# The experts' result rows, stored by ScalarE's DMA queue two units later instead of by GpSimd's

## The reference, cut to what matters

```python
def _hier_moe(h, w_rg, b_rg, w_re, b_re, w1, w3, w2):
    ...
    e_id = g_top[:, None] * EXPERTS_PER_GROUP + top_j
    combine = jnp.einsum('nk,nke->ne', w_sel,
                         jax.nn.one_hot(e_id, N_EXPERTS, dtype=jnp.float32)).astype(h.dtype)
    y = jnp.zeros_like(hf)
    for e in range(N_EXPERTS):
        he = jax.nn.silu(hf @ w1[e]) * (hf @ w3[e])
        y = y + combine[:, e:e + 1] * (he @ w2[e])
    return y.reshape(B, S, D)

    # in second_block:
    x = x + g2[:, None, :] * _hier_moe(h2, w_rg[l], b_rg[l], w_re[l], b_re[l], w1[l], w3[l], w2[l])
```

## Time and profile before

| | us |
|---|---|
| median of 3 runs | 2029.37 |
| lowest and highest | 2022.58 and 2034.13 |
| the profiled execution's own time | 2036.26 |
| its span in the trace | 2034.5 |
| TensorE busy in the span | 1849.5 |
| the experts' stage, first group load to the last gather | about 1737 to 2026 |

### The profile page before, as it was taken

One profiled execution on the slowest core, in us unless ns is written; L12 is line 12 of the kernel. 1 busy time (PEld: TensorE's weight loads), 2 busy tenths in 40 slices (PEclk: granted clock), 3 DMA queues, 4 the chain that ended last, 5 costly groups with the idle time before them and its releaser, 6 DMA issues.

```text
span 2034.5 us, 16531 instructions
## 1 busy us (share of the span) xinstructions
PE 1849.5 (91%) x6558; PEld 1022.6 (50%) x6558; DVE 730.0 (36%) x1289; ACT 246.5 (12%) x519; POOL 114.3 (6%) x121
## 2 busy tenths in 40 slices
PE   6999879989999999998899989999798667799997
PEld 1454368644555444446455768844474554233332
DVE  0384253346677201022322256500336854211112
ACT  2000221110000000001022211100121130101110
POOL 0000000010000000001000000000202210100001
PEclk9999965799999999999756799999899768799999
DMA  9353400023646421127100048944342313999997
GB/s 347 123 194 137 167 21 1 0 103 124 223 170 227 165 83 65 59 83 269 57 0 1 1 148 326 332 165 155 82 166 83 114 60 127 352 391 387 390 392 283
DMA packets 160684, 334.45 MB, mean 164 GB/s; under 512 B 15192, under 2 KB 15472, under 8 KB 160608
## 3 DMA queue, kind: packets, MB, share of 16 engines
q1 hardware_dynamic: 141408, 298.87, 40.3%
q0 software_dynamic: 18288, 31.37, 4.8%
q10 hardware_dynamic: 912, 3.17, 0.4%
HBM read 355.58 MB, written 15.48 MB: 182 GB/s over the span
## 4 chain that ended last, share of the span: by engine, by line
PE 82%; DVE 9%; DMA 3%; issue 2%; ACT 2%; POOL 1%; SPq 0%; DVEq 0%; POOLq 0%; ACTq 0%
PE psum L535 79%; PE psum L539 4%; DMA wring<-in_w_mod 1%; POOL small L1220 1%; ACT big L1351 1%; DMA y_slots<-lnb 1%; DMA wring<-in_mlp_w 1%; ACT wide L1351 1%; DVE big L1875 0%; DVE small L1729 0%; DVE xres L1736 0%; DVE big L2015 0%; DVE big L2034 0%; DVE wide L1700 0%; DVE small L2033 0%
## 5 line engine op out<-in xcount | busy, mean ns | idle before, releaser
L535 PE MATMUL psum<-wring,big 128*128 128x512 f32 (+1 forms) x1536 | 559.4, 598 | 13.0 <-issue 10.2
L535 PE MATMUL psum<-wide,wring 128*128 128x256 f32 (+1 forms) x1520 | 513.8, 486 | 5.0 <-DVE wide L1700 5.0
L535 PEld LDWEIGHTS psum<-wring,big 128*128 128x128 f32 (+1 forms) x1536 | 231.6, 173 | 326.1 <-issue 326.1
L535 PEld LDWEIGHTS psum<-wide,wring 128*128 128x128 f32 x1520 | 276.2, 190 | 131.9 <-issue 112.0
L1662 DVE SCALAR_TENSOR_TENSOR wide<-wring,csilu,wide 128x512 f32<-128x512 f32 x364 | 250.4, 749 | 3.0
L535 PE MATMUL psum<-wring,wide 128*128 128x512 f32 (+2 forms) x512 | 208.2, 554 | 0.0
L535 PE MATMUL psum<-big 128*128 128x64 f32 (+3 forms) x480 | 131.6, 451 | 27.7 <-DVE big L1932 9.1
L1714 DVE TENSOR_TENSOR wide<-psum,gate 128x512 f32<-128x512 f32 x28 | 19.4, 692 | 377.9 <-PE psum L535 377.9
L535 PE MATMUL psum<-big,wide 128*64 128x512 f32 (+2 forms) x568 | 137.0, 544 | 3.9 <-DVE wide L1798 3.9
L535 PEld LDWEIGHTS psum<-const,wide 128*128 128x128 f32 x480 | 88.8, 199 | 95.3 <-issue 85.1
L1351 ACT ACTIVATE big<-psum 128x512 f32<-128x512 f32 (+1 forms) x141 | 76.1, 541 | 490.3 <-PE psum L535 369.7
(11 more groups left out here) (252 smaller groups left out, 1026.2 us busy)
## 6 DMA issues: line engine op xcount, KB each, us to landing
wring<-in_mlp_w SPq DMA_DIRECT2D x32, 2048.0 KB, 8.1
wring<-in_w SPq DMA_DIRECT2D x32, 2048.0 KB, 21.2
wring<-in_w_mod SPq DMA_DIRECT2D x24, 2048.0 KB, 10.2
big<-in_w SPq DMA_DIRECT2D x23, 2048.0 KB, 20.7
wide<-in_w SPq DMA_DIRECT2D x14, 2048.0 KB
wring<-in_w_ada SPq DMA_DIRECT2D x12, 2048.0 KB, 8.8
wring<-in_w_in SPq DMA_DIRECT2D x8, 2048.0 KB, 8.4
wring<-in_ev_w_in SPq DMA_DIRECT2D x6, 2048.0 KB, 13.5
```

The costliest lines, as they stand in the source:

```text
L535: return nc.tensor.matmul(o, a, b, start=first, stop=last)
```

## The change

The store leaves GpSimd's program and stands in ScalarE's, after the Silu of place i and for place i-2. GpSimd is left with the 12 group loads one after the other, the wait for all stores and the four gathers. The view that is stored, the semaphores and the number of stores (21) stay.

```diff
@@ GpSimd @@
-            begins = sorted(BEGINS)
-            loaded = 0
-            for i in range(UNITS - LATE):
-                while loaded < GROUPS and (loaded < 2 or begins[loaded - 2] <= i + 1):
-                    load_group(loaded)
-                    loaded += 1
-                u = ORDER[i]
-                pool.wait_ge(ysb_ready, i + 1)
-                pool.dma_start(y_slots[u * SLOTS:(u + 1) * SLOTS, :].rearrange("s (n c) -> n s c", n=2),
-                               ysb[:, i % 2, :]).then_inc(y_stored[i % 2], 16)
-            assert loaded == GROUPS
+            for n in range(GROUPS):
+                load_group(n)
             for a in range(2):
                 pool.wait_ge(y_stored[a], 16 * ((UNITS - LATE + 1 - a) // 2))
@@ ScalarE @@
+            def store_y(i):
+                u = ORDER[i]
+                act.wait_ge(ysb_ready, i + 1)
+                act.dma_start(y_slots[u * SLOTS:(u + 1) * SLOTS, :].rearrange("s (n c) -> n s c", n=2),
+                              ysb[:, i % 2, :]).then_inc(y_stored[i % 2], 16)
+
             act.wait_ge(pick_turned, 1)
...
                 act.wait_ge(up_done, i + 1)
                 f(sg[:, i % 2, :], psum[:, i % 2, 0:T], ACT.Silu).then_inc(sg_ready, 1)
+                if i > 1:
+                    store_y(i - 2)
                 if i + 1 in BEGINS:
                     modulate_group(BEGINS[i + 1])
```

## The result

| | before | after |
|---|---|---|
| median of 4 runs, us | 2029.86 | 2112.93 |
| lowest and highest | 2022.58, 2034.13 | 2098.50, 2122.75 |
| profiled execution, own time | 2036.26 | 2122.75 |
| its span | 2034.5 | 2120.9 |

The ratio is 1.0407, with a 95% interval of 1.034 to 1.0475: 83 us slower, where 98 were forecast. Ratios in this document leave out executions in a slow state of the chip; that is one of all, of 6354.78 us, in the run with GpSimd's late stores. The two profiled executions are 86.4 us apart in their spans. Of this the experts' stage begins 1.2 us later, which the change has no part in: the first group load is issued at 1738.08, before at 1736.91.

A forecast was written before the change was run, and what follows sets the result against it. DMA engines, mostly moving weights, and TensorE were both nearly used up. The pair's extra load +92.7, less 2.7, tail +8, made +98 on the profiled 2036.3 us; median forecast 2127 us, range 2085 to 2155.

The forecast's parts named there:

- The bound: Experts' stage: DMA engines and TensorE both nearly used up; work added to one or two DMA engines counts in full.
- Two engines, always the same pair: Stores on ScalarE's queue: outer dimension 2 gives two DMA engines, the same every time; chance 0.80, 2127 us.
- GpSimd's and ScalarE's sides: Experts' stage: GpSimd loses 21 issues, worth 0; ScalarE's 21 waits and issues of 0.41 to 1.59 us are hidden, 0.
- Rival (b): ScalarE's store issues are blocked while SyncE's queue is full: 24 us in all, 2053; chance 0.03.
- VectorE's side: `keep_y` waits for store i-2 with 14.5 us left: 0; in mid-stage a late store delays only VectorE.
- The sum: Experts' stage: net 2.26 MB more on the pair at 24.4 GB/s, +92.7 us, less 2.7 saved on GpSimd's queue: +90.
- The tail: After the last Silu: the last store lands late on the pair, gathers begin at T+12.4 instead of T+4.1: +8 us.
- (a): ScalarE's stores move round or spread over all sixteen engines: -1 to +2 us, 2026 to 2030; chance 0.13.
- (c): The pair is fixed, but has spare speed when fourteen engines idle, or gets less load: 2085 to 2105; chance 0.04.

The follow-up runs named there:

- the run with GpSimd's late stores: Kernel before, stores still on GpSimd's queue, but each waits until `up` of two units later is done: 2033.2 us, ratio 1.0048.
- The series 2, 4, 8, 64: Changed kernel, store's outer dimension 2 (ratio 1.0407), 4 (1.0207; forecast extra 40 us, less 3), 8 (1.0032; forecast 14, less 3), 64 as two DMAs (0.9966).
- the windows at the quiet end: Kernel before, its two output stores at outer dimension 2; profiled: both on ScalarE's queue 2055.1 us, ScalarE's plus SyncE's 2054.2, both on GpSimd's 2030.5.
- the run with halves: Changed kernel, each store still on ScalarE's queue but issued as two DMAs of 64 partitions: 2021.2 us, ratio 0.9966 to before.
- The two output stores on GpSimd's queue: Kernel before, its two output stores given outer dimension 2 and issued by GpSimd's queue: 2030.5 us in the profiled execution.

## Why the prediction was right, and where it was off

*The bound.* Right. What was left of the weights at 2090 lay on the pair; work on two engines counted almost in full while the mean share fell to 0.80.

*Two engines, always the same pair.* Right, and that it is the same pair could only be bounded before. The series 2, 4, 8, 64 and the windows at the quiet end show both halves. One reading behind it was weaker than it looked: I gave the share of 0.14 in the window 2014 to 2015 to the store alone. The DMA view of that microsecond splits it into 7.5% for GpSimd's queue and 7.0% for weights:

```profile
q0 software_dynamic: 15, 0.03, 7.5%
q1 hardware_dynamic: 8, 0.03, 7.0%
```

The count of two engines held, but that window couldn't prove it for a store; the quiet end of the kernel does.

*GpSimd's and ScalarE's sides.* Right at 0 for ScalarE: its issues took 0.50 us, and doubling their number cost nothing that can be measured. The free group loads gained nothing visible. Rival (b) is out by the row of ScalarE's issues: an issue is not held up although SyncE's take 9.4 us at the median.

*VectorE's side.* The cost was right, its reason was not. I expected a store to land in 8 to 13 us, inside 14.5. Fourteen of the 21 stores kept VectorE waiting for its buffer, and from their issue to the end of that wait it was 17.3 to 21.3 us. For store 19, issued at 2080.24, the chain has it:

```profile
2080.24 17.28 DMA y_slots<-lnb
```

The equal packet counts at 2090 explain most of it. While weights are queued, a store's 131,072 bytes on an engine pass together with twice as many of weights: 3 x 131,072 bytes at 25.6 GB/s are 15.4 us, an estimate from the rows above. VectorE waited 87.2 us. It cost nothing in the middle for the other reason that I had given: TensorE waited longer for weights.

*The sum: the term that was mis-sized is the pair's speed.* Expected +90 to the end of the last Silu, measured +77.7. I let the pair run at 24.4 GB/s an engine, a sixteenth of 390. Alone it makes 26 (0.13 and 52 GB/s above). In the stage the pair moved by my count 5.42 + 2.26 MB in 222.4 + 77.7 = 300.1 us: 25.6 GB/s, and somewhat more if the last w1 and w3 landed well ahead of 2083.45. The same speed puts four engines at (5.42+0.98)/25.6 = 250 us, +28, and eight at +3. Measured are +32.6 and +4.8 in the length of the stage. Of my 40 and 14, less 3 each, it is nearer for eight; for four it is as far below as 37 is above. The period points the same way: 49.4 us for two experts where I had 51. While all sixteen were busy they made 24.4 each, and even in the run with halves 394/16 = 24.6; what they lose together stays open, as does what the change saved on GpSimd's queue, where I had put 2.7 us.

*A term that the sum didn't have: TensorE's clock.* Each long wait is followed by a slow stretch. After the last, of 9.49 us, the granted clock was 0.54 over 6.6 us, so mostly the lower of the two levels, and 16 products took 6.64 us where they took 3.60 before:

```profile
2069.60:2076.20 6.60, 6.60 (x17) 1.94 (x17) 0.00 (x0) 0.00 (x0) 0.00 (x0) 0.54 0.86 298
```

In the middle the next wait for weights takes this up. Behind the last it doesn't: TensorE is busy without a gap from 2076.6 to the last Silu, so some 3 us of the 77.7 are the clock's.

*The tail.* +8 expected, +7.4 measured.

*The rivals.* (a) was the mechanism of the run with halves, and its time, 2026 to 2030, was a little too high: 2021. The 3 us that it took for GpSimd's own cost are nearer to 6, the change in the stage's length. (c), a pair with spare speed, is what the 25.6 GB/s are a mild form of.

## What to carry to other kernels

Before a DMA is moved from GpSimd's queue to ScalarE's or SyncE's, look at the outer dimension of its view in device memory: here one that began with 2 ran on two engines, and on these queues on the same two every time. In a stage that waits for loads spread over all engines, the price was its bytes divided by 2 at some 25.6 GB/s, for every one of them, and the mean DMA share fell, it didn't rise. Two DMAs with 64 rows outside cost 0.5 us of issue each and took all of it away.

## What the runs showed of the hardware that was not expected

A two-engine store on GpSimd's queue carries about 430 packets under 512 bytes with it, and the stage takes 269.6 and 270.3 us without them, on either queue, where it took 275.6. How much of that is the packets and how much the uneven load of a pair that moves round, no run tells apart. On ScalarE's queue the same store has none of them but its completions: 939 in the whole stage after the change. The two output stores on GpSimd's queue, of twice the bytes, brought 912 each, 1690 of the 1824 between 2012 and 2016 with only 0.18 MB beside them, and that is where the 13.7 us in place of 8 to 11 may come from (DMA view of 2010 to 2028.7):

```profile
DMA packets 2080, 1.06 MB, mean 56 GB/s; under 512 B 1824, under 2 KB 1824, under 8 KB 2080
```

ScalarE's and SyncE's queues share one pair of engines for such stores, and the pair gives both queues the same number of packets. A store of 2 KB packets beside weights of 4 KB packets so got a third of the pair's bytes.

TensorE's granted clock was 0.87 over the slowed stage and 1.00 over the same work before. It fell in each wait of 9.5 to 13.5 us for weights (0.62 over 1813.0 to 1826.3, the first of them) and was back at 1.00 once the 16 products behind the wait were done. In the middle that cost nothing that shows, at the end some 3 us.
